# Up projections of a two-layer feed-forward with 512 moving columns, and their scale multiplied on GpSimd

## Time and profile before

| | us |
|---|---|
| median of three runs | 2883.1 |
| the profiled execution, device time | 2885.24 |
| its span, first to last instruction | 2883.4 |
| first up run after its lead to the down run's first matmul | 440.97 to 787.00 |
| first down run | 787.00 to 967.91 |
| second up run after its lead | from 1328.92 |
| PE busy, share of the span | 97% |
| DVE, ACT, POOL busy | 66%, 48%, 13% |

### The profile page before, as it was taken

The page is one execution under the profiler, slowest core; times in us unless marked ns, Lnnn a source line. Parts: engine busy times, 40 slices in busy tenths (PEclk is TensorE's granted clock), DMA queues, the critical chain, the costliest instruction groups (busy, mean ns, idle before and its releaser), DMA issues.

```text
span 2883.4 us, 54264 instructions
## 1 busy us (share of the span) xinstructions
PE 2792.3 (97%) x20454; PEld 2616.2 (91%) x20454; DVE 1899.2 (66%) x2829; ACT 1378.7 (48%) x1931; POOL 375.1 (13%) x344
## 2 busy tenths in 40 slices
PE   8999999999999999989999999999999999999998
PEld 8998889999988899889999988899878889987887
DVE  4585567666655687668666655586667766676775
ACT  4434555444543457445444443453345454334553
POOL 0060022222211000021222211000000010000001
PEclk9999999999999999999999999999999999999999
DMA  6455445555555454344555555444444455444454
GB/s 227 162 168 183 139 139 176 187 178 186 179 189 187 141 176 154 132 147 147 187 178 186 179 188 188 154 161 162 159 146 156 161 188 164 163 158 149 151 168 139
DMA packets 131916, 481.75 MB, mean 167 GB/s; under 512 B 14768, under 2 KB 14896, under 8 KB 131632
## 3 DMA queue, kind: packets, MB, share of 16 engines
q1 hardware_dynamic: 130608, 475.06, 50.0%
q10 hardware_dynamic: 1152, 4.47, 0.4%
HBM read 477.38 MB, written 2.10 MB: 166 GB/s over the span
## 4 chain that ended last, share of the span: by engine, by line
PE 89%; DVE 5%; ACT 3%; POOL 2%; issue 1%; DMA 1%; ACTq 0%; DVEq 0%; POOLq 0%
PE BANK L450 52%; PE BANK L455 16%; PE BANK L456 8%; PE BANK L471 7%; DVE WLO L1293 2%; ACT WHI L879 1%; PE BANK L522 1%; PE BANK L827 1%; PE BANK L817 1%; PE BANK L462 1%; DMA TB<-tab 1%; PE BANK L676 1%; DVE TM L1885 0%; POOL M L2000 0%; DVE TM L1315 0%
## 5 line engine op out<-in xcount | busy, mean ns | idle before, releaser
L450 PE MATMUL BANK<-H,WHI 128*128 128x256 f32 x8256 | 1518.5, 286 | 33.1 <-DVE H L1303 29.6
L1293 DVE TENSOR_TENSOR WLO<-RING,WHI 128x1024 fp32r<-128x1024 f32 x902 | 1115.4, 1239 | 629.7 <-ACT WHI L879 623.1
L879 ACT ACTIVATE WHI<-RING 128x1024 fp32r<-128x1024 f32 x902 | 950.4, 1055 | 937.6 <-PE BANK L450 415.7
L450 PEld LDWEIGHTS BANK<-H,WHI 128*128 128x128 f32 x8256 | 1300.8, 193 | 43.3 <-issue 35.4
L450 PE MATMUL BANK<-H,WLO 128*128 128x256 f32 x4128 | 1173.3, 284 | 0.0
L450 PEld LDWEIGHTS BANK<-H,WLO 128*128 128x128 f32 x4128 | 797.7, 193 | 0.0
L455 PE MATMUL BANK<-BIGR,WHI 128*128 128x512 f32 x1536 | 543.0, 399 | 3.6 <-DVE BIGR L1913 3.6
L456 PE MATMUL BANK<-BIGR,WLO 128*128 128x256 f32 x1536 | 431.4, 281 | 0.0
L455 PEld LDWEIGHTS BANK<-BIGR,WHI 128*128 128x128 f32 x1536 | 288.6, 188 | 75.8 <-DVE BIGR L1913 4.2
L456 PEld LDWEIGHTS BANK<-BIGR,WLO 128*128 128x128 f32 x1536 | 290.2, 189 | 0.0
L471 PE MATMUL BANK<-WHI,H 128*128 128x512 f32 x640 | 213.7, 403 | 1.7 <-DVE BIG L1391 1.7
(11 more groups left out here) (279 smaller groups left out, 2272.3 us busy)
## 6 DMA issues: line engine op xcount, KB each, us to landing
RING<-w SPq DMA_DIRECT2D x902, 512.0 KB, 3.3
X<-xT ACTq DMA_DIRECT2D x4, 512.0 KB, 10.0
TB<-tab ACTq DMA_DIRECT2D x1, 1536.5 KB, 16.5
outT<-M SPq DMA_DIRECT2D x3, 512.0 KB, 2.9
V<-vec ACTq DMA_DIRECT2D x1, 644.0 KB, 18.7
outT<-M SPq DMA_DIRECT2D x2, 256.0 KB, 3.2
BIG<-pos ACTq DMA_DIRECT2D x1, 128.0 KB, 3.5
V<-vec ACTq DMA_DIRECT2D x1, 8.0 KB, 6.8
```

The costliest lines, as they stand in the source:

```text
L450: last = mm(bank[:, 0:T], wt[s][:, kk, :], x, start=start and n == 0, stop=stop and n == 2)
L879: A(WHI[at % SPLIT][:, :, :], RING[at % RAW][:, :].rearrange("p (k n) -> p k n", k=UB), ACT.Copy)\
L1293: TT(WLO[at % SPLIT][:, :, :], RING[at % RAW][:, :].rearrange("p (k n) -> p k n", k=UB), WHI[at % SPLIT][:, :, :].bitcast(f32), ALU.subtra ...
```

```
-        FFN = {l: [Run(64, KT, "f", "H", "ffn", l), ...
+        FFN = {l: [Run(64, KT, "f", "H", "ffn", l, wide=True), ...
@@ ACT step
-                        for m in range(BANKS):
+                        for m in range(BANKS - 1):
                             tap(0, m)
...
-                        tap(i, j)
+                        tap(i, j - 1)
...
-                    if r.kind == "ffn" and j % 2:
-                        gelu(i, j)
+                    if r.kind == "ffn" and j % 2 == 0:
+                        gelu(i, j - 1)
...
                 groups(act, c, r, step, beside and beside(l, o0), led)
+                if r.kind == "ffn":
+                    tap(r.n // BANKS, -1)
+                    gelu(r.n // BANKS, -1)
@@ DVE scaled, step
-                    if r.wide:
-                        both(y, bank).then_inc(sem("bank_free"), 1)
-                        dve.wait_ge(sem("bank_free"), i * BANKS + (o0 + j + 1))
-                        TT(y, y, RS[:, :], ALU.mult).then_inc(sem("y_scaled"), 1)
-                    else:
-                        TT(y, bank[:, 0:T], RS[:, :], ALU.mult).then_inc(sem("bank_free"), 1)
+                    both(y, bank).then_inc(sem("bank_free"), 1)
...
                     if r.kind == "ffn":
-                        taps(i, j)
+                        taps(i, j - 1)
...
                 groups(dve, c, r, step, beside and beside(l, o0), led)
+                if r.kind == "ffn":
+                    taps(r.n // BANKS, -1)
@@ POOL run
+                    def scaled(i, j):
+                        y = TM[:, 8 + j, :]
+                        pool.wait_ge(sem("bank_free"), i * BANKS + (o0 + j + 1))
+                        g.tensor_tensor(y, y, RS[:, :], ALU.mult).then_inc(sem("y_scaled"), 1)
+
+                    def step(i, j):
+                        scaled(i, j)
+                        if j % 2 == 0:
+                            gate(i, j // 2 - 1)
+
+                    for j in range(BANKS):
+                        scaled(0, j)
+                    gate(0, 0)
+                    groups(pool, c, r, step, led=BANKS)
+                    gate(r.n // BANKS, -1)
```

More of the change, by code:

```diff
@@ L142, in __init__ @@
                 self.tail = last or kind == "m"
-        FFN = {l: [Run(64, KT, "f", "H", "ffn", l), Run(16, FF_T, "f", "HID", "m", wide=True)] for l in (0, 1)}
+        FFN = {l: [Run(64, KT, "f", "H", "ffn", l, wide=True), Run(16, FF_T, "f", "HID", "m", wide=True)] for l in (0, 1)}
         RUNS_INDEX = [Run(9, KT, "f", "H", "f", AB_QI), Run(2, KT, "v", "H", "v", AB_WI)]
@@ L394, in groups @@
                 step(m // BANKS, m % BANKS)
+        first = sum(r.n for r in (*RUNS_INDEX, RUN_U, RUN_Q, POOL_RUN, RUN_K, RUN_V, RUN_POOLED, RUN_HEADS))
+        second = sum(r.n for r in (*FFN[0], RUN_C, RUN_X, Q_RUN, KN_RUN, KV_RUN, LRU_RUN, RUN_Y, RUN_LRU, FIRST_HEADS, LAST_HEADS))
+        UP_OUTPUTS = first, first + second
         SUMMED_ADDED = (1, 3, 5, 7, 9, 10)
@@ L1006, in step @@
                         tick(c)
-                    if r.kind == "ffn" and j % 2:
-                        gelu(i, j)
+                    if r.kind == "ffn" and j % 2 == 0:
+                        gelu(i, j - 1)
                 def tap(i, j):
-                    if r.wide:
-                        act.wait_ge(sem("y_scaled"), i * BANKS + (2 * p0 + j + 1))
-                    else:
-                        act.wait_ge(sem("bank_free"), i * BANKS + (o0 + j + 1))
+                    act.wait_ge(sem("y_scaled"), i * BANKS + (2 * p0 + j + 1))
                     if j % 2 == 0 and least(i) * 2 + p0 + j // 2 >= 2:
                         act.wait_ge(sem("gated"), i * 2 + (p0 + j // 2 - 1))
-                    A(TM[:, j, :], TM[:, 8 + j, :], ACT.Identity, scale=vcol("ffn_w", i * BANKS + (192 * r.dst + 128 + j)),
+                    A(TM[:, j % BANKS, :], TM[:, 8 + j % BANKS, :], ACT.Identity, scale=vcol("ffn_w", i * BANKS + (192 * r.dst + 128 + j)),
                       bias=vcol("ffn_b", i * BANKS + (64 * r.dst + j))).then_inc(sem("tap"), 1)
@@ L1024, in gelu @@
                         act.wait_ge(sem("gated"), pair - 1)
-                    A(TM[:, 4 + j // 2, :], TM[:, j - 1, :], ACT.Gelu_apprx_tanh).then_inc(sem("gelu_done"), 1)
+                    A(TM[:, 4 + j // 2 % 2, :], TM[:, (j - 1) % BANKS, :], ACT.Gelu_apprx_tanh).then_inc(sem("gelu_done"), 1)
                 groups(act, c, r, step, beside and beside(l, o0), led)
+                if r.kind == "ffn":
+                    tap(r.n // BANKS, -1)
+                    gelu(r.n // BANKS, -1)
                 if r.kind == "add":
```

15 lines of the change are left out of this document (5 added, 10 removed).

## The result

The changed kernel takes 2861.0 us (median; its executions lie from 2854.2 to 2871.1) against 2883.95 (2882.6 to 2885.0) of the kernel before in the same series. The ratio is 0.9923, interval 0.9908 to 0.9938: 23.0 us or 0.8% faster, where the prediction said 11.1 and its range ended 8 us above the time that came.

The account below looks back on a forecast made before the run. PE issuing its matmuls was taken as the bound. Per layer 346.03 - (339.2 + 1.3) = 5.5 us plus 0.05 from the lead, 11.1 for both: 2883.1 - 11.1 = 2872.0 us, range 2869 to 2876.5, chance 0.80.

Parts of the forecast that it names:

- The price of a wide block: PE's up runs: 353.3 ns a block instead of 359.8, over 960 blocks 6.8 us less a layer.
- The lead: Start of the up run: normalizing `X` sets the pace, so only its last unit gains, 0.05 us.
- The wait behind the lead: PE waits about 1.3 us for a late low, instead of 0.12; bounds nothing and 4.0 us.
- The loop: Up run's loop: highs and lows have 5 us to spare, so PE's waits there are put at nothing.
- Turn-taking of DVE and POOL: Both reading SBUF take turns: 10.2 of 11.3 us per pair of outputs; each POOL operation costs DVE up to 0.53.
- The rival in which DVE becomes the bound: Up run's loop: DVE needs 12.2 us a pair, over 11.5, giving 2925 us; chance 0.04.
- The end of the run: Last remainder about 8.2 us after the last output instead of 5.7, ACT's first high about 6.5; nothing added.
- No wait: Rival: PE has no wait behind the lead, 6.8 us less a layer, 2869.4 us; chance 0.08.
- Half of what the down run shows: Rival: a dropped matmul saves half, wide block 356.5 ns, up run gains 2.5 us, 2878.1 us; chance 0.03.
- The rule of the Trainium skill: PE's matmuls: isolated gap of N/2.4 + 2.5 ns, so a gain of 2.5 ns a block, 2.4 us a layer.

Follow-up runs that it names:

- the repeat: The changed kernel, unaltered, run again against the kernel before: 2864.4 us, ratio 0.9933.
- the kernel with the early unit: The changed kernel with ACT's rounding and DVE's remainder of the unit PE waits for behind the lead made one step earlier: 2861.1 us, ratio 0.9927.
- the kernel that is wide alone: The kernel before with wide up runs; DVE sums and scales, taps, gelu and gating stay where they were: 2901.1 us, ratio 1.0058.
- the one with the moves alone: The changed kernel with the narrow product; DVE copies the bank, GpSimd scales, taps, gelu and gating one output later: 2884.0 us, ratio 1.0000.
- the run without the waits: The changed kernel with the 15th and 16th unit of the up run made ahead on ACT and DVE: 2860.9 us, ratio 0.9921.

## Why the prediction was right in direction and wrong in size

**The price of a wide block** is the step that failed. The prediction took 353.3 ns from the down run, found 354 at a second place, and used it as the only value. In the trace of before 346.5 stood 59 us further on. What the runs showed in its place are two prices, 353.3 and 346.7 ns, of which each long stream takes one. The up run's stream goes on into the down run, so a draw of 346.7 is worth 9.4 us a layer, not only in the 960 blocks that were changed. The median of the first series, 11 us below the forecast, is that of executions in which one or both streams have the lower price (9.4 us each), as the traces show: one such stream in the repeat, two in the kernel with the early unit. The unprofiled executions themselves have no trace. That the profiled one came within 3 us of the forecast gain is the draw of both streams at 353.3, and luck as far as the size goes. Where both streams drew 353.3, the sum is close: 5.5 us a layer were forecast, and 5.8 came in the first and, with 0.4 us of the 12.1 falling between the layers, 5.9 in the second. The mechanism was right; the term needed two values and a chance for each. As a dropped instruction, the saving is 360.0 - 353.3 = 6.7 or 360.0 - 346.7 = 13.3 ns a block.

**The lead** was mis-sized: 0.05 us forecast, 0.43 measured. "The normalizing of `X` sets that pace" was a misreading. This is PE's chain in the changed kernel's lead, two rounds of a block for four outputs and the token sums behind them:

```profile
424.23 0.86 PE BANK L525 x4
...
427.87 0.86 PE BANK L525 x4
```

The round takes 3.64 us in place of 3.73. 2.87 us of products and 0.86 of sums are 3.73: PE was busy all the time, and the 0.86 that the prediction took for waiting were matmuls with ones.

**The wait behind the lead**: 1.3 us forecast, 1.63 measured and two slips of 0.1 behind it (at 459.12 and 462.07). The path is the one described. DVE's four sums take 2.48 us (forecast 2.44), and the low that PE waits for starts at 457.28 and takes 1.38:

```profile
443.27 2.48 DVE L1301 TENSOR_REDUCE TM<-BANK 128x256 f32<-128x512 f32 x4
...
455.01 0.84 DVE L1406 SCALAR_TENSOR_TENSOR TM<-TM,V 128x254 f32<-128x254 f32 x1
...
457.28 1.38 DVE L1296 TENSOR_TENSOR WLO<-RING,WHI 128x1024 fp32r<-128x1024 f32 x1 [1.43 <-ACT WHI L882]
```

The prediction had 0.3 us of turn-taking on this path; here the tap takes 0.84 in place of 0.48 and the low 1.38 in place of 1.23, 0.5 in all. Both waits together were forecast at 2.6 us and are worth 3.8 to 4.7; that this is the place where the rate of 1415 blocks is drawn was not seen.

**The loop**: no waits, as forecast. POOL's multiplication takes 0.91 us (forecast 1.2), POOL is 130 us busier (forecast about 110).

**Turn-taking of DVE and POOL** is there, and in the loop it costs what it was said to cost, nothing on PE's path. DVE's second tap went from 483 to 710 ns, POOL's rounding from 1174 to 1438 (0.40 us where DVE is idle). These are the rows of before in 460 to 787:

```profile
L1971 POOL CAST BIGR<-TM 128x256 f32 x29 | 34.1, 1174 | 4.9 <-POOL TM L1969 4.9
L1408 DVE SCALAR_TENSOR_TENSOR TM<-TM,V 128x254 f32<-128x254 f32 x58 | 28.0, 483 | 8.1 <-DVE TM L1406 0.2
```

Only who pays was different: the lows, which were to be lengthened most, take 1221 ns (1243 before). The rival in which DVE becomes the bound did not occur here; it came, by another way, in the kernel that is wide alone.

**The end of the run**: last remainder forecast 8.2 us behind the last output, ACT's first high 6.5. In POOL's and ACT's timeline, against 781.24:

```profile
787.26 0.73 POOL L1977 TENSOR_TENSOR BIGR<-TM,BIGR 128x256 fp32r<-128x256 f32 x1
```

```profile
787.32 1.99 ACT L882 ACTIVATE WHI<-RING 128x1024 fp32r<-128x1024 f32 x2
```

That is 6.8 and 6.1, and PE goes on without a gap.

**The rivals.** "No wait" gave 2869.4; it was nearer only because its sum was lower, since the waits are there. It is wrong, as all the others, in the block's price. "Half of what the down run shows" (356.5 ns) is refuted by 353.3 and 346.7. The rule of the Trainium skill (TensorE: Matmul & The Clock Gate, "Back-to-back issue gap") that gave 2.5 ns for a dropped instruction is off by more than the prediction said: the traces give 6.7 or 13.3. The page gives it for an isolated matmul, and these are streams.

**What stays open.** What in a pause decides the rate, and whether GpSimd's multiplication without the later taps would have been enough. In the traces, the streams that follow narrow blocks directly (the down runs of the kernel before and of the one with the moves alone, 4 of 4) run at 353.3, those right behind the last sums of a lead (14 in 7 traces) at 346.7, and those behind a late low at either. Inside the leads the rounds of eight blocks behind the sums run at either as well, so the sums alone do not fix it. No stream of 24 blocks or more changed its rate without a slip in its starts, the smallest being the 0.015 us in the kernel that is wide alone. That a pause sets a phase between weight loads and matmuls that the alternating stream keeps, and the 512, 256, 256, 512 order doesn't, is only argued, and the traces do not show it: the recorded weight loads start 2 to 4 ns behind the start of the matmul before them at either rate.

## What to carry to other kernels

A matmul's price in a long stream is to be read at several places of the trace, behind different starts, before one value goes into a sum: here it had two, 2% apart, which a stream of 1415 blocks keeps to its end. When executions of one kernel spread in steps, count the matmuls per 100 us in each long stretch at full granted clock; if the counts differ, vary the order of long and short matmuls. And a wide form that saves TensorE an instruction pays only if the work behind each bank (sum, scale, taps) is not a row of steps that wait for each other: here one output of delay took the waits out, and the second engine saved a further 1 us a layer.

## What was not expected of the hardware

- Blocks of a 512- and a 256-column matmul, each with its weight load, run at 346.7 or 353.3 ns when strictly alternating, at 348.3 in the order 512, 256, 256, 512, and three matmuls of 256 at 360.0 ns, all at a granted clock of 1.00.
- A slip of PE of 0.1 us, and once of 0.015, came with a change of the rate, which can be worth 9.4 us behind it; slips of 0.03 and 0.06 us in the trace of the run without the waits left it as it was.
- Where DVE and POOL both read SBUF, a rounding of POOL took 1.17 us (before) and 1.44 (changed) in place of the 0.40 it takes beside an idle DVE, and the changed kernel's second tap of DVE 0.71 in place of 0.48, while DVE's large subtractions stayed at 1.22.
